# A two-block transformer kernel on one core: norm boundaries taken one row block at a time

## The chip, the cores and the metric

The kernel runs on one core of a Trainium2 chip. The metric is the device time of one execution in microseconds (us). TensorE (PE) does the matrix products, VectorE (DVE), ScalarE (ACT) and GpSimd (POOL) the rest, and SyncE (SP) issues the loads of weights.

## The reference, cut to what matters

Two blocks run one after the other on an x of 512 tokens by 1024 features, all in float32. Each has projections, mixers, gates and a projection back onto the residual. The change touches what stands between them, the root-mean-square norms:

```python
def rms_norm(x, g):
    xf = x.astype(jnp.float32)
    y = xf * lax.rsqrt(jnp.mean(xf * xf, axis=-1, keepdims=True) + EPS)
    return (y * g.astype(jnp.float32)).astype(x.dtype)

# first block
h = rms_norm(x, g_pre_mix);  ...            # "norm1"
x = x + rms_norm(merged @ w_o, g_post_mix)  # post norm "post1"
hf = rms_norm(x, g_pre_ffn)                 # "norm2"
f_gate, f_up = jnp.split(hf @ w_ffn_in, 2, axis=-1)
f = (jax.nn.silu(f_gate) * f_up) @ w_ffn_out
x = x + rms_norm(f, g_post_ffn)             # post norm "post2"
# second block, for l in 0, 1
h = rmsnorm(x, norm_w) * (1.0 + scale[:, None, :]) + shift[:, None, :]   # "layer"
...
x = x + gate[:, None, :] * (merged @ w_out)
# behind it
return rmsnorm(x, final_norm_w)             # "final"
```

## The kernel before

Everything is written out by hand, with semaphores; each engine runs its instructions strictly in the order of the code. A matrix product of float32 accuracy is made of three passes over rounded high parts and low remainders. A weight panel of 1024 by 512 comes as two halves into `raw`. For each half ScalarE makes the high part (`split_hi`, 128x2048) and VectorE the remainder (`split_lo`, 128x2048, semaphore `w_lo`); `w_lo` releases both TensorE and the next load into that half.

The tokens lie in four row blocks of 128 (`tb` 0 to 3). `xres` holds x, and `row0` (shown as R) the rows on their way through a norm. PSUM has eight banks, used as two sets: set 0 is banks 0 to 3, set 1 banks 4 to 7. `set_free[S]` tells TensorE that a set may be written again.

There are four boundaries that the change touches. In the text they are called **A** (`w_o`, then `norm2`), **B** (`ffn_down`, then the first `layer.norm`), **C** (`w_out` of layer 0, then `layer.norm` of layer 1) and **D** (`w_out` of layer 1, then the final norm and the output). At each, TensorE finishes the second 512 columns of a product bank by bank (the order is called `stagger`: banks of blocks 0 and 1, then, after the first halves of blocks 2 and 3, those of blocks 2 and 3). At A and B each row block then goes through this chain between ScalarE and VectorE (`post_norm`, once for each engine):

1. half square sum of the product (`second_half` on ScalarE; at B VectorE first adds up the product in `stage`, `second_half` on VectorE),
2. its mean (`post_variance`, L1137), its root on ScalarE (`post_root`, L655), and beside it the gain (`second_gained`),
3. reciprocal and residual addition (`post_add`, L1146 and L1147, 128x1024),
4. square sum of x (`post_square`, L627), mean (`variance`, L1112), root (`root`, L632), reciprocal (`inverse`, L1118),
5. scaled rows into `row0` (`scaled`, L637, semaphore `xn_ready`).

At C and D the chain is shorter: `update` (two VectorE instructions, L1738 and L1739), half square (`second_half`, L650), mean (L1137), root, inverse, scaled. The split of one more weight half (`split_hi(c.g + 2, 0)` and `split_lo(c.g + 2, 0)`) stands in the middle of each chain. On TensorE `norm_transposes` (L1871) turns the scaled rows: 8 transposes of 128x128 for each block, 4 into each set. Behind them ScalarE reads the banks (`norm_hi` L644 at A, `modulated` L971 at B and C) from the first transpose of block 3 on (the eighth from the end), since `rows_done` counts those of block 3. At D VectorE multiplies the scaled rows with the gain (L1768) and SyncE writes them out.

Two waits of `norm_transposes` matter: at A, set 1 is given free only behind the whole `post_norm` of VectorE; at B, set 0 by `second_half(3)` of VectorE and set 1 long before; at C, set 1 behind `update(1, 3)`.

## Time and profile before

| | before |
|---|---|
| median of 3 runs | 2818.04 us (2817.92 to 2820.89) |
| the profiled execution | 2815.42 us |
| its span, first to last instruction | 2813.7 us |
| PE busy | 2662.9 us, 95% |
| DVE busy | 1210.3 us, 43% |
| ACT busy | 973.6 us, 35% |
| mean granted clock of TensorE | 0.972 of full |

The span is what the trace covers; the execution's own time is 1.7 us more. A busy TensorE is the rule here, so the stretches in which it stands still are the ones to look at.

### The profile page before, as it was taken

The numbers are of one execution on the slowest core, as the hardware profiler recorded it, in microseconds if no ns is written. First come the engines' busy times: TensorE is split into PE (matmuls) and PEld (weight loads), VectorE is DVE, ScalarE is ACT, GpSimd is POOL, SyncE is SP. The second block draws the span as 40 slices with busy tenths as digits, with TensorE's granted clock in tenths as the row PEclk, the third lists the DMA queues.
The fourth block names the chain that finished last, engine by engine and source line by source line (L and its number), as shares of the span: only waits on it lengthen the run. The fifth ranks groups of instructions, "written<-read, shape, count | busy, mean of one in ns | idle before, by whom it ended". The sixth has DMA issues, their size and how long they took to land.

```text
span 2813.7 us, 34747 instructions
## 1 busy us (share of the span) xinstructions
PE 2662.9 (95%) x13629; PEld 2246.0 (80%) x13629; DVE 1210.3 (43%) x1592; ACT 973.6 (35%) x1244; POOL 406.5 (14%) x433
## 2 busy tenths in 40 slices
PE   7999999999997999997999999998999999999897
PEld 6887778777886888886888888987778888888785
DVE  5445555545534655525233333442343332443334
ACT  6335443145324212114333332222343333322233
POOL 3013344000000000000301002321030000123200
PEclk9989999999998999998999999999999999999998
DMA  5220003312431554422322232212222222322221
GB/s 209 75 75 16 16 6 112 105 64 90 149 120 60 183 186 169 149 90 68 112 90 89 89 112 96 93 66 90 75 85 96 89 95 89 128 73 89 80 94 55
DMA packets 43488, 269.26 MB, mean 96 GB/s; under 512 B 5304, under 2 KB 5424, under 8 KB 16000
## 3 DMA queue, kind: packets, MB, share of 16 engines
q1 hardware_dynamic: 31536, 226.51, 23.4%
q0 software_dynamic: 11280, 39.31, 4.1%
q10 hardware_dynamic: 576, 2.10, 0.2%
q8 instruction: 68, 1.11, 0.2%
q14 instruction: 28, 0.23, 0.0%
HBM read 265.80 MB, written 2.10 MB: 95 GB/s over the span
## 4 chain that ended last, share of the span: by engine, by line
PE 68%; issue 19%; DVE 6%; POOL 4%; ACT 3%; DMA 0%; DVEq 0%; POOLq 0%; ACTq 0%
PE PS L1775 66%; POOL merged L578 1%; DVE w_split L1090 1%; PE PS L1981 1%; ACT w_split L614 1%; POOL res_hi L572 1%; POOL res_lo L572 1%; POOL merged L517 1%; DVE small L1335 0%; PE PS L1871 0%; DVE R L1423 0%; DVE h_act L1098 0%; DVE xres L1147 0%; ACT R L627 0%; POOL R L601 0%
## 5 line engine op out<-in xcount | busy, mean ns | idle before, releaser
L1775 PE MATMUL PS<-h_act,w_split 128*128 128x512 f32 x5472 | 1262.1, 392 | 12.2 <-DVEq L1102 7.2
L1775 PEld LDWEIGHTS PS<-h_act,w_split 128*128 128x128 f32 x5472 | 1033.3, 189 | 229.5 <-issue 5.6
L1090 DVE TENSOR_TENSOR w_split<-raw,w_split 128x2048 fp32r<-128x2048 f32 x215 | 508.7, 2366 | 981.0 <-ACT w_split L614 964.8
L614 ACT ACTIVATE w_split<-raw 128x2048 fp32r<-128x2048 f32 x215 | 411.6, 1915 | 835.2 <-PE PS L1775 828.1
L1775 PE MATMUL PS<-w_split,h_act 128*128 128x256 f32 (+2 forms) x2496 | 429.2, 325 | 24.9 <-DVE h_act L1098 19.9
L1775 PEld LDWEIGHTS PS<-w_split,h_act 128*128 128x128 f32 x2496 | 359.1, 193 | 54.3 <-DVE h_act L1098 14.0
L1775 PE MATMUL PS<-y_act,w_split 128*128 128x512 f32 x1152 | 265.2, 391 | 2.2 <-DVE w_split L1090 2.2
L1775 PEld LDWEIGHTS PS<-y_act,w_split 128*128 128x128 f32 x1152 | 217.3, 189 | 47.8 <-DVE w_split L1090 2.6
L1775 PE MATMUL PS<-R 128*128 128x128 f32 (+3 forms) x896 | 189.4, 362 | 9.7 <-ACT R L997 5.5
L1775 PEld LDWEIGHTS PS<-R 128*128 128x128 f32 x896 | 134.3, 200 | 41.6 <-issue 15.0
L1775 PE MATMUL PS<-w_split,res_hi 128*128 128x384 f32 x512 | 130.6, 336 | 0.0
L1775 PE MATMUL PS<-w_split,y_act 128*128 128x512 f32 x528 | 122.5, 394 | 7.8 <-DVE y_act L1098 6.9
L1775 PEld LDWEIGHTS PS<-w_split,y_act 128*128 128x128 f32 x528 | 100.0, 190 | 30.4 <-issue 5.7
L517 POOL TENSOR_TENSOR merged<-merged,small 128x256 f32<-128x256 f32 (+2 forms) x96 | 88.3, 920 | 222.1 <-DVE small L1344 221.8
L578 POOL TENSOR_TENSOR merged<-merged,small 128x768 f32<-128x768 f32 x32 | 46.3, 1469 | 473.5 <-DVE small L1637 473.5
L818 ACT ACTIVATE merged<-PS,small 128x128 f32<-128x128 f32 (+3 forms) x128 | 66.9, 525 | 108.1 <-DVE small L1335 108.1
L614 ACT ACT_TABLE_LOAD x22 | 28.2, 1283 | 207.7 <-PE PS L1775 207.7
L697 ACT ACTIVATE stage<-PS 128x512 f32<-128x512 f32 x94 | 56.0, 598 | 108.2 <-PE PS L1775 108.0
L1775 PEld LDWEIGHTS PS<-w_split,res_hi 128*128 128x128 f32 x512 | 92.0, 188 | 0.0
L1335 DVE TENSOR_REDUCE small<-PS 128x2 f32<-128x256 f32 (+2 forms) x96 | 57.7, 601 | 69.0 <-PE PS L1775 68.6
L1775 PE MATMUL PS<-w_split,res_lo 128*128 128x384 f32 x256 | 85.6, 334 | 0.0
L572 POOL TENSOR_TENSOR res_hi<-h_act,cf 128x512 fp32r<-128x512 f32 x16 | 28.6, 1786 | 333.8 <-DVE h_act L1098 333.8
(274 smaller groups left out, 2143.4 us busy)
## 6 DMA issues: line engine op xcount, KB each, us to landing
raw<-in_weights SPq DMA_DIRECT2D x214, 1024.0 KB, 4.9
R<-in_w_ada POOLq DMA_DIRECT2D x36, 512.0 KB, 4.8
gate_bc<-in_w_ada POOLq DMA_DIRECT2D x12, 512.0 KB, 4.6
xres<-in_x ACTq DMA_DIRECT2D x4, 512.0 KB, 5.6
R<-in_nsa_wk POOLq DMA_DIRECT2D x1, 2048.0 KB, 10.3
xres<-in_x POOLq DMA_DIRECT2D x1, 2048.0 KB, 10.8
R<-in_decay POOLq DMA_DIRECT2D x8, 256.0 KB, 2.9
out<-R SPq DMA_DIRECT2D x4, 512.0 KB, 3.0
```

The source lines that it names most:

```text
L517: pool.tensor_tensor(probs, probs, nsa_fac[:, u % 4, 0:n].unsqueeze(2).to_broadcast([P, n, nk]), ALU.mult).then_inc(p_ready, 1)
L572: pool.tensor_tensor(residue_tiles[part][kt].rearrange("p (r i) -> p r i", r=RES), source, ones, ALU.mult).then_inc(residues_ready, 1)
L578: pool.tensor_tensor(Pa[r], Pa[r], fac[:, r:r + 1].to_broadcast([P, 768]), ALU.mult).then_inc(a_p, 1)
L614: act.activation(w_split[:, 0, half, :, :], raw[:, half, :, :], ACT.Copy).then_inc(w_hi, 1)
L697: act.activation(stage[:, slot0 + j, :], PS[:, 4 * S + j, :], func).then_inc(staged, 1)
L818: last = act.activation(Pn[:, u % 3, k * nk:(k + 1) * nk], PS[:, 4 + u % 2, k * nk:(k + 1) * nk], ACT.Exp, bias=nsa_nmx[:, u % 4, k:k + 1] ...
L1090: dve.tensor_tensor(w_split[:, 1, half, :, :], raw[:, half, :, :], w_split[:, 0, half, :, :].bitcast(F32), ALU.subtract).then_inc(w_lo, 1)
L1335: dve.reduce_max(nsa_nmx[:, u % 4, 0:n], PS[:, 4 + u % 2, 0:n * (qb + 1) * P] .rearrange("p (b k) -> p b k", b=n), AX, negate=True).then_i ...
L1775: return pe.matmul(out, lhsT, rhs, start=start, stop=stop, skip_group_check=True)
L1981: last = pe.transpose(PS[:, 6, k * P:(k + 1) * P], Pn[:, u % 3, k * P:(k + 1) * P], ident)
```

## The change

On ScalarE a root of one spare element (`root_table`) stands ahead of each chain. Both chains now take block 0 to the end of its residual addition before block 1 begins, and blocks 2 and 3 likewise. `split_lo(c.g + 2, 0)` becomes two instructions of 128x1024: the first in the old place, the second behind the last residual addition. In `norm_transposes` only blocks 0 and 1 are written to one set before the other; blocks 2 and 3 are each written to both. The parameter `first` is never passed.

```diff
+            def root_table():
+                act.activation(spare, cf[:, C_ONE:C_ONE + 1], ACT.Sqrt)
...
             def post_norm(posts, k, rows, second_half, ahead):
 
+                root_table()
                 second_half(0)
+                post_root(posts, 0)
                 second_half(1)
-                post_root(posts, 0)
+                post_square(posts, 0)
                 post_root(posts, 1)
-                post_square(posts, 0)
+                root(k, 0)
+                scaled(rows, 0)
                 post_square(posts, 1)
-                root(k, 0)
                 root(k, 1)
-                scaled(rows, 0)
+                scaled(rows, 1)
                 ahead()
-                scaled(rows, 1)
                 second_half(2)
                 post_root(posts, 2)
+                post_square(posts, 2)
                 second_half(3)
                 post_root(posts, 3)
-                post_square(posts, 2)
                 root(k, 2)
+                scaled(rows, 2)
                 post_square(posts, 3)
-                scaled(rows, 2)
                 root(k, 3)
                 scaled(rows, 3)
...
+                root_table()
                 second_half(0)
+                root(k, 0)
                 second_half(1)
-                root(k, 0)
+                scaled(rows, 0)
                 root(k, 1)
-                scaled(rows, 0)
                 scaled(rows, 1)
                 split_hi(c.g + 2, 0)
...
+            def split_lo_part(g, half, part):
+                two = slice(2 * part, 2 * part + 2)
+                dve.wait_ge(w_hi, 2 * g + half + 1)
+                ins = dve.tensor_tensor(w_split[:, 1, half, two, :], raw[:, half, two, :],
+                                        w_split[:, 0, half, two, :].bitcast(F32), ALU.subtract)
+                if part:
+                    ins.then_inc(w_lo, 1)
...
-            def post_norm(own, posts, k, rows, second_half, second_gained, ahead):
+            def post_norm(own, posts, k, rows, second_half, second_gained, g):
 
                 second_half(0)
-                second_half(1)
                 post_variance(posts, 0)
                 second_gained(0)
+                post_add(own, posts, 0)
+                second_half(1)
                 post_variance(posts, 1)
                 second_gained(1)
-                post_add(own, posts, 0)
+                variance(rows, 0)
                 post_add(own, posts, 1)
-                variance(rows, 0)
+                inverse(k, rows, 0)
                 variance(rows, 1)
-                inverse(k, rows, 0)
                 inverse(k, rows, 1)
-                ahead()
+                split_lo_part(g, 0, 0)
                 second_half(2)
                 post_variance(posts, 2)
                 second_gained(2)
                 post_add(own, posts, 2)
                 second_half(3)
                 post_variance(posts, 3)
+                variance(rows, 2)
                 second_gained(3)
-                variance(rows, 2)
                 post_add(own, posts, 3)
+                split_lo_part(g, 0, 1)
                 inverse(k, rows, 2)
                 variance(rows, 3)
                 inverse(k, rows, 3)
...
                 update(1, 0, x_ready)
+                mean(0)
+                inverse(k, rows, 0)
                 update(1, 1, x_ready)
-                mean(0)
                 mean(1)
-                inverse(k, rows, 0)
                 inverse(k, rows, 1)
-                split_lo(c.g + 2, 0)
+                split_lo_part(c.g + 2, 0, 0)
                 update(1, 2, x_ready)
                 mean(2)
                 inverse(k, rows, 2)
                 update(1, 3, x_ready)
+                split_lo_part(c.g + 2, 0, 1)
                 dve.sem_inc(set_free[1], 1)
                 mean(3)
                 inverse(k, rows, 3)
...
-            def norm_transposes(c, rows):
+            def norm_transposes(c, rows, first=0):
...
-                for S in range(2):
+                for S in (first, 1 - first):
                     pe.wait_ge(set_free[S], (c.u0, c.u1)[S])
-                    for tb in range(TB - 1):
+                    for tb in range(2):
                         pe.wait_ge(xn_ready, rows + tb + 1)
                         row(tb, S)
-                pe.wait_ge(xn_ready, rows + TB)
-                row(TB - 1, 0)
-                row(TB - 1, 1)
+                for tb in range(2, TB):
+                    pe.wait_ge(xn_ready, rows + tb + 1)
+                    row(tb, 0)
+                    row(tb, 1)
```

Three places in the order of instructions. First ScalarE at B, from the block-0 and block-1 part's end to the last scaled rows. Before (L614 is `split_hi`, L961 the half square, L655 `post_root`, L627 `post_square`, L632 `root`, L637 `scaled`):

```order
L614 ACTIVATE w_split<-raw 128x2048
L637 ACTIVATE R<-xres,small 128x1024
L961 ACTIVATE merged,small<-stage 128x512
L655 ACTIVATE small<-small 128x1
L961 ACTIVATE merged,small<-stage 128x512
L655 ACTIVATE small<-small 128x1
L627 ACTIVATE R,small<-xres 128x1024
L632 ACTIVATE small<-small 128x1
L627 ACTIVATE R,small<-xres 128x1024
L637 ACTIVATE R<-xres,small 128x1024
L632 ACTIVATE small<-small 128x1
L637 ACTIVATE R<-xres,small 128x1024
```

Of the change (L615, L966, L656, L628, L633 and L638 are the same in this order):

```order
L638 ACTIVATE R<-xres,small 128x1024
L615 ACTIVATE w_split<-raw 128x2048
L966 ACTIVATE merged,small<-stage 128x512
L656 ACTIVATE small<-small 128x1
L628 ACTIVATE R,small<-xres 128x1024
L966 ACTIVATE merged,small<-stage 128x512
L656 ACTIVATE small<-small 128x1
L633 ACTIVATE small<-small 128x1
L638 ACTIVATE R<-xres,small 128x1024
L628 ACTIVATE R,small<-xres 128x1024
L633 ACTIVATE small<-small 128x1
L638 ACTIVATE R<-xres,small 128x1024
```

The split moved behind the scaled rows of block 1; the 128x1024 square of block 2 stands ahead of the half square of block 3, and the scaled rows of block 2 ahead of the square of block 3.

Then VectorE at B, from `second_half(3)` (L1597) to the last reciprocal. Before (L1603 is `second_gained`):

```order
L1597 TENSOR_TENSOR stage<-PS,R 128x512
L1137 SCALAR_TENSOR_TENSOR small<-small 128x1
L1603 TENSOR_TENSOR R<-stage,R 128x512
L1112 TENSOR_SCALAR small<-small 128x1
L1146 RECIPROCAL small<-small 128x1
L1147 SCALAR_TENSOR_TENSOR xres<-R,small,xres 128x1024
L1118 RECIPROCAL small<-small 128x1
L1112 TENSOR_SCALAR small<-small 128x1
L1118 RECIPROCAL small<-small 128x1
```

Of the change (L1614 is `second_half`, L1620 `second_gained`, L1163 the residual addition, L1104 `split_lo_part`, L1134 `inverse`):

```order
L1614 TENSOR_TENSOR stage<-PS,R 128x512
L1153 SCALAR_TENSOR_TENSOR small<-small 128x1
L1128 TENSOR_SCALAR small<-small 128x1
L1620 TENSOR_TENSOR R<-stage,R 128x512
L1162 RECIPROCAL small<-small 128x1
L1163 SCALAR_TENSOR_TENSOR xres<-R,small,xres 128x1024
L1104 TENSOR_TENSOR w_split<-raw,w_split 128x1024
L1134 RECIPROCAL small<-small 128x1
L1128 TENSOR_SCALAR small<-small 128x1
L1134 RECIPROCAL small<-small 128x1
```

The second half of the weight split stands between the last residual addition and the reciprocal of block 2, and the mean of block 2 moved ahead of the gain of block 3.

Last TensorE in `norm_transposes` of a layer (B and C); register rows are the waits on `xn_ready`. Before:

```order
L1871 MATMUL PS<-cf,R 128x128 x4
L1877 REGISTER_ALU
L1871 MATMUL PS<-cf,R 128x128 x4
L1877 REGISTER_ALU
L1871 MATMUL PS<-cf,R 128x128 x4
L1875 REGISTER_ALU
L1871 MATMUL PS<-cf,R 128x128 x12
L1879 REGISTER_ALU
L1871 MATMUL PS<-cf,R 128x128 x8
```

Of the change:

```order
L1889 MATMUL PS<-cf,R 128x128 x4
L1895 REGISTER_ALU
L1889 MATMUL PS<-cf,R 128x128 x4
L1893 REGISTER_ALU
L1889 MATMUL PS<-cf,R 128x128 x8
L1898 REGISTER_ALU
L1889 MATMUL PS<-cf,R 128x128 x8
L1898 REGISTER_ALU
L1889 MATMUL PS<-cf,R 128x128 x8
```

Before, set 0 takes blocks 0, 1 and 2 (4, 4 and 4), then set 1 takes the same three (12), then block 3 goes into both (8). Now set 0 takes blocks 0 and 1 (4 and 4), set 1 the same two (8), and blocks 2 and 3 go into both sets, each behind its own wait (8 and 8).

## Rows read from the trace of the kernel before

**Rows 1.** The page: busy time of each engine.

```profile
PE 2662.9 (95%) x13629; PEld 2246.0 (80%) x13629; DVE 1210.3 (43%) x1592; ACT 973.6 (35%) x1244; POOL 406.5 (14%) x433
```

**Rows 2.** The transposes L1871: idle us and times before them, by what ended it.

```profile
  ACT R L637: 31.0, 8
```

**Rows 3.** Timeline at A: start us, us, engine, line, operation [idle before].

```profile
884.38 1.28 ACT L655 ACT_TABLE_LOAD   x1
...
885.67 0.30 ACT L655 ACTIVATE small<-small 128x1 f32<-128x1 f32 x2
...
891.42 1.90 ACT L614 ACTIVATE w_split<-raw 128x2048 fp32r<-128x2048 f32 x1
...
893.35 2.29 DVE L1090 TENSOR_TENSOR w_split<-raw,w_split 128x2048 fp32r<-128x2048 f32 x1 [2.69 <-ACT w_split L614]
...
895.63 0.68 DVE L1511 TENSOR_TENSOR R<-PS,R 128x512 f32<-128x512 f32 x1
...
895.86 0.58 ACT L932 ACTIVATE merged<-PS 128x512 f32<-128x512 f32 x1
...
898.04 1.04 ACT L627 ACTIVATE R<-xres 128x1024 f32<-128x1024 f32 x1
...
899.54 1.28 DVE L1147 SCALAR_TENSOR_TENSOR xres<-R,small,xres 128x1024 f32<-128x1024 f32 x1
...
903.10 4.74 PE L1871 MATMUL PS<-cf,R 128*128 128x128 f32 x24 [7.71 <-ACT R L637]
903.17 0.17 DVE L1118 RECIPROCAL small<-small 128x1 f32<-128x1 f32 x1 [0.98 <-ACT small L632]
903.37 1.15 ACT L637 ACTIVATE R<-xres,small 128x1024 f32<-128x1024 f32 x1 [0.23 <-DVE small L1118]
907.03 4.74 ACT L644 ACTIVATE h_act<-PS,vecs 128x512 fp32r<-128x512 f32 x8 [2.51 <-PE PS L1871]
...
910.88 4.38 PE L1775 MATMUL PS<-h_act,w_split 128*128 128x512 f32 x12 [3.04 <-DVEq L1102]
```

**Rows 4.** Timeline at B.

```profile
1303.91 1.89 ACT L614 ACTIVATE w_split<-raw 128x2048 fp32r<-128x2048 f32 x1
...
1308.05 0.68 DVE L1597 TENSOR_TENSOR stage<-PS,R 128x512 f32<-128x512 f32 x1
...
1312.67 1.96 PE L1871 MATMUL PS<-cf,R 128*128 128x128 f32 x8 [9.22 <-DVEq L1600]
...
1315.07 1.28 DVE L1147 SCALAR_TENSOR_TENSOR xres<-R,small,xres 128x1024 f32<-128x1024 f32 x1
...
1318.63 5.17 PE L1871 MATMUL PS<-cf,R 128*128 128x128 f32 x24 [4.00 <-ACT R L637]
...
1322.56 2.79 ACT L971 ACTIVATE R<-PS,mod_cols 128x512 f32<-128x512 f32 x4 [2.51 <-PE PS L1871]
```

**Rows 5.** Timeline at C.

```profile
2041.54 16.62 PE L1775 MATMUL PS<-w_split,h_act 128*128 128x512 f32 x72 [0.96 <-DVE w_split L1090]
...
2053.33 1.90 ACT L614 ACTIVATE w_split<-raw 128x2048 fp32r<-128x2048 f32 x1
...
2057.47 0.68 DVE L1738 TENSOR_TENSOR stage<-PS,gate_bc 128x512 f32<-128x512 f32 x1
...
2061.50 1.96 PE L1871 MATMUL PS<-cf,R 128*128 128x128 f32 x16 [2.46 <-ACT R L637]
...
2064.60 2.79 ACT L971 ACTIVATE R<-PS,mod_cols 128x512 f32<-128x512 f32 x4 [0.42 <-PE PS L1871]
...
2067.69 5.68 PE L1775 MATMUL PS<-h_act,w_split 128*128 128x512 f32 x17 [2.36 <-ACTq L619]
```

**Rows 6.** Timeline at D.

```profile
2805.24 0.16 DVE L1118 RECIPROCAL small<-small 128x1 f32<-128x1 f32 x1 [0.27 <-ACT small L632]
...
2805.50 4.63 DVE L1768 TENSOR_TENSOR R<-R 128x1024 f32<-128x1024 f32 x4
```

**Rows 7.** Stretch at C: us, busy (instructions) of PE, PEld, DVE, ACT, POOL, PEclk, DMA.

```profile
2068.00:2069.00 1.00, 1.00 (x3) 0.81 (x3) 1.00 (x4) 1.00 (x3) 0.00 (x0) 0.50 0.00 0
```

7 lines of the change are left out of this document (4 added, 3 removed).

## The prediction

> **What bounds the kernel now.** I read the page first: TensorE is busy for 2662.9 us, 95% of the span [rows 1], so only what shortens the stretches in which it stands still, or the tail behind it, can show. Then the view of the transposes L1871: TensorE idled 31.0 us ahead of them, eight times, until scaled rows (L637) came [rows 2]. That is the sum over the norms and all that is to be had there, about 1% of the span. Then the timelines of the four boundaries, which show what is last. At A the scaled rows of block 2 let a run of 24 transposes begin at 903.10, after 7.71 us of idle time, and ScalarE reads the first finished bank at 907.03 [rows 3]. At B the run of 24 begins at 1318.63 and the first read is at 1322.56 [rows 4]. In both, 16 transposes stand ahead of those of block 3 in this run, and with the first of block 3 they take 3.93 us (907.03 - 903.10, and the same at B). At C a run of 16 takes 1.96 us from 2061.50, and the read is at 2064.60 [rows 5]. At D, the end of the program, VectorE starts its four products at 2805.50, as soon as its last reciprocal (2805.24) is done [rows 6]. So at A, B and C the first read of block 3's banks sets when the next product starts; at D the last reciprocal does.
>
> I take the prices from these rows. An element-wise pass of VectorE over 128x1024: 4.63 / 4 = 1.16 us [rows 6]. Split of a whole weight half on VectorE 2.29, on ScalarE 1.90; half square 0.58 and about 0.12 for its accumulator; gain 0.68; addition to x 1.28; square 1.04 and about 0.11; reciprocal 0.17; scaled rows 1.15; root 0.30 / 2, with hand-over 0.2 [rows 3]. Overlaps of 0.1 and hand-overs of 0.04 are put in as the rows have them. Walking the old order with these prices gives the old starts within 0.15 us at all four places, so I walk the new order the same way.
>
> **The change part by part.**
>
> **Table load.** It goes from behind the second half square (884.38 at A) to ahead of the first, where ScalarE waits for TensorE anyway. Once the load of 1.28 us has begun at 884.38 the roots begin at 885.67, so 1.29 us are freed and nothing beyond the load [rows 3]. They are worth something only if blocks 0 and 1 bound what follows. At A they don't: the split of ScalarE stood between the scaled rows of blocks 0 and 1 and now stands behind both, so it starts at 891.22 by my walk, against 891.42. At B the block-wise order even delays it. `second_half(1)` is now queued behind the addition of block 0 on VectorE, the square of block 0 behind `second_half(1)` on ScalarE, and each reciprocal behind the next addition: the split starts at 1305.98 against 1303.91 [rows 4]. At C it can't start before the first halves of TensorE's banks are done; 48 products behind 2041.54 at 16.62 / 72 = 0.231 each that is 2052.6, against 2053.33 [rows 5]. The Trainium skill ("ScalarE: Activation LUTs", section "What ACT_TABLE_LOAD costs") puts a switch at 2.66 us, as the load and a drain behind it of about 1.38. This case's trace does not agree: the root follows the load directly. By the page each of four boundaries could give 1.38 us more, 5.5 in all.
>
> **Weight split in two.** 2.29 becomes 1.16 + 1.16 (+0.03 in sum), and blocks 2 and 3 begin 1.13 us earlier after ScalarE's part. The rest comes behind the last addition. At A: `post_variance(2)` 1.1 us earlier (894.4). At C: `update(1, 2)` starts at 2055.65 against 2057.47, by 0.7 from the split of ScalarE and 1.13 from here. At B: 2.07 late and 1.13 early, so `second_half(2)` starts at 1309.05 against 1308.05 [rows 4].
> `w_lo` comes later by 3.5 us (C) to 10 us (B). The next product reads it behind the transposes: at 910.88 at A, where it comes by 902.0; at C 2067.69 against 2061.0. Only the load of the next panel's first half is queued on SyncE's ring behind it, and that half is first touched by ScalarE after 48 more products (11 us) of the group that follows. I cost both at nothing; without that cover the lateness itself would be paid.
>
> **Tail of the chain, A and B.** This is the part that costs. On ScalarE the square of block 2 (waiting for the addition) is now ahead of the half square of block 3, which ran during the wait before. Behind the last addition there came: square 3, its mean, root, reciprocal, scaled rows of block 3. Now there come: half a split 1.16, reciprocal of block 2, scaled rows of block 2 (1.15), and only then square 3 (1.15), mean, root, reciprocal.
> At A: addition 2 starts at 895.3, the square of block 2 at 896.64, and the half square of block 3 moves from 895.86 to 897.7; so addition 3 starts at 899.55, as before (899.54); half a split to 902.0; reciprocal 2 to 902.1; scaled 2 to 903.25; square 3 to 904.3; mean, root and reciprocal to 904.95. Before, that reciprocal ended at 903.34 [rows 3]. It is the point at which set 1 is given free, so at A the new order of the transposes gives nothing: 8 of set 1, 8 of block 2 and the first of block 3 are again 17 behind it, 3.93 us, so the read is at 908.9 against 907.03. A: **+1.9**.
> At B: addition 3 starts at 1315.8 (before 1315.07), reciprocal 2 is at 1318.2, scaled 2 to 1319.5, square 3 to 1320.55, reciprocal 3 to 1321.2, scaled 3 to 1322.35 (before 1320.05). But here set 1 has long been free, so the 8 of set 1 go into idle time from 1315.3 on, the 8 of block 2 are done by 1321.4, and the first of block 3 runs at once: read at 1322.35 + 0.5 = 1322.85 against 1322.56 [rows 4]. B: **+0.3**. Of 3.93 us of transposes saved, all but 0.5 are spent on the later chain.
>
> **Tail at C and D.** Everything from `update(1, 2)` on is 1.8 us earlier; the second half split delays the last mean by 0.3. At C set 1 is given free behind that split, at 2060.95; 17 transposes at 1.96 / 16 = 0.12 and the first's latency of 0.25 make 2063.3 against 2064.60 [rows 5]. C: **-1.25**. At D the last reciprocal, and with it the four products and the output, come 1.8 - 0.3 = 1.5 earlier [rows 6]. D: **-1.5**.
>
> At norm1 the transposes run in one piece with all rows ready; nothing changes. TensorE's clock is taken as it is: after the restart at C it is granted 0.50, the 1.2 GHz level [rows 7], and 17 products took 5.68 us instead of 17 x 0.231 = 3.93 [rows 5]; at A 12 took 4.38 instead of 2.77, and the 24 transposes 4.74, 0.20 each against 0.12 at C [rows 3, 5]. So a restart costs about 1.7 us at the low level, and I leave that cost where it is.
>
> **Sum:** 1.9 + 0.3 - 1.25 - 1.5 = -0.55 us, so the profiled execution goes from 2815.42 to 2814.9. The median of the runs is 2.6 us above that execution; I carry it over: 2818.04 - 0.55 = 2817.5.
>
> **The rivals.** A measurement of this kernel tells about 0.2% (5.6 us) from no change.
>
> *The forecast, small losses at A and B against small gains at C and D.* Own range: an error of 0.5 in each of the four walks, and the run-to-run spread of 1.5: 2815.5 to 2819.5. Chance 0.78.
>
> *The tails do not lengthen (faster).* If square 3 still came right behind addition 3, the end would keep its old distance from that addition. A would be 0 (899.55 against 899.54). B would be 0.73 late (1315.8 against 1315.07), scaled 3 done at 1320.8 and the read at 1321.3 against 1322.56, -1.3. With C and D that is -4.0: 2814.0. The queues speak against it: on ScalarE scaled 2 stands ahead of square 3 and waits for a reciprocal behind the half split. With the page's 5.5 on top it would be 2808.5, for which nothing in the rows speaks. Chance 0.07, of which 0.03 beyond 0.2%.
>
> *The clock of TensorE (slower).* The idle time at A grows from 7.71 to 9.6 us, and at C a gap of 2.46 us gives way to one that is placed differently, while the transposes come in more pieces. If the low level then lasts twice as long at the three restarts, each pays 1.7 us more: -0.55 + 5.1 = +4.6, 2822.6; if also the transposes of C (24, now at 0.12 each) ran at 0.21 (5.17 / 24 at B), +1.7 to +2 more, over the 0.2% bound. It decides from one restart on (1.7 against 0.55). For it speaks that the level is 0.50 after the gap at C [rows 7]; against it, that the transposes of A and B run at the slow pace already. The Trainium skill's "TensorE: Matmul & The Clock Gate", section "HAM oscillation", tells the same way round: gaps bring the clock down and the restart pays at half rate. Chance 0.12, of which 0.03 beyond 0.2%.
>
> *The opposite at the clock*, one restart of C at the full level: -1.75 more, 2815.7; it lies in the range. Chance 0.03.
>
> So faster 0.04, same 0.92, slower 0.04. The range for 8 in 10, with half of the clock case in it: 2815.0 to 2820.5.
>
> **What would show it.** Right: at A the run of transposes (24 in one) begins 1.9 us later than before, measured from the end of the product; at B 8 more transposes directly behind the first 8, and the first read within 0.5 of before; at C that read 1.25 earlier; at D the four products 1.5 earlier behind the product; table loads ahead of the first half square with nothing waiting. Wrong: a half square of block 3 that still overlaps addition 2; a half split that takes well over 1.2 us; a wait on `w_lo` at a restart; or more products at the low pace behind a restart than the 12 at A and the 17 at C.

## The result, and the profile after

The changed kernel takes 2822.61 us in the median of 20 runs (2819.78 to 2824.67), the kernel before 2818.01 us in 20 runs (2815.19 to 2820.89). The ratio is 1.0016, with a 95% interval of 1.0009 to 1.0023: 4.6 us slower, a small loss that the interval separates from no change, inside the 0.2% that the prediction named. The forecast of 2817.5 us is off by 5.1 us, and 2822.61 lies above the range of 2815.0 to 2820.5. The profiled execution took 2821.88 us with a span of 2820.2, against 2815.42 and 2813.7. Of those 6.5 us in span 2.5 stand ahead of 632 us, a part that varies by up to 3 us between two traces of one kernel (see the last section). Behind it the change costs 4.0 us, and these are what has to be explained.

The page, and the view of the transposes (now L1889), with what ended TensorE's idle time ahead of them:

```profile
PE 2668.0 (95%) x13613; PEld 2249.6 (80%) x13629; DVE 1210.4 (43%) x1596; ACT 975.2 (35%) x1248; POOL 406.4 (14%) x433
```

```profile
  DVEq L1531: 18.5, 2
  ACT R L638: 11.7, 6
...
  DVEq L1617: 10.1, 1
```

The idle time moved from the scaled rows [rows 2] to other releasers, among them VectorE's queue at A (L1531, 9.11 us at A itself) and at B (L1617). PE shows 5.1 us more busy time than in [rows 1] for the same products. A TensorE that does the same work in more busy time is a first sign of its clock.

The four boundaries are measured from a common start, so that what lies ahead of them doesn't count. At B, C and D it is the start of the product's second panel, ahead of which TensorE stands still for 0.96 us. At A the products run on without a break, so the start is that of the first eight transposes, which follow the last product at once. In the kernel before:

```profile
894.35 1.03 PE L1871 MATMUL PS<-cf,R 128*128 128x128 f32 x8
```

In the changed kernel they start at 896.89, 2.54 us later. Its timeline at A (start us, us, engine, line, operation, idle time before):

```profile
877.84 1.28 ACT L663 ACT_TABLE_LOAD   x1
...
896.89 1.04 PE L1889 MATMUL PS<-cf,R 128*128 128x128 f32 x8
...
900.03 0.58 ACT L937 ACTIVATE merged<-PS 128x512 f32<-128x512 f32 x1
...
901.78 1.28 DVE L1163 SCALAR_TENSOR_TENSOR xres<-R,small,xres 128x1024 f32<-128x1024 f32 x1
902.99 1.22 DVE L1104 TENSOR_TENSOR w_split<-raw,w_split 128x1024 fp32r<-128x1024 f32 x1
...
904.31 1.15 ACT L638 ACTIVATE R<-xres,small 128x1024 f32<-128x1024 f32 x1 [3.09 <-DVE small L1134]
...
907.04 5.38 PE L1889 MATMUL PS<-cf,R 128*128 128x128 f32 x24 [9.11 <-DVEq L1531]
...
910.97 4.74 ACT L645 ACTIVATE h_act<-PS,vecs 128x512 fp32r<-128x512 f32 x8 [2.67 <-PE PS L1889]
...
914.82 2.55 PE L1793 MATMUL PS<-h_act,w_split 128*128 128x512 f32 x10 [2.40 <-DVEq L1118]
```

It is the order that the prediction walked. The half square of block 3 (900.03) stands behind the square of block 2, and the last addition (901.78), half a split (902.99), the scaled rows of block 2 (904.31) and the square of block 3 (at 905.37) follow one another. The 24 transposes begin at 907.04 in one run and the first read is at 910.97. Less 2.54 that is 908.43, against 907.03 [rows 3]: **+1.4**, where +1.9 was forecast. The table load (877.84) stands ahead with nothing waiting.

This late read costs nothing in the end. TensorE restarts 1.40 us late (914.82 less 2.54 is 912.28, against 910.88 [rows 3]), but at the full clock. The first 5 us behind the restart, before and after (us, busy time and number of instructions of PE, PEld, DVE, ACT and POOL, granted clock, DMA share, GB/s):

```profile
910.88:915.88 5.00, 5.00 (x16) 4.03 (x17) 4.75 (x6) 2.68 (x3) 0.54 (x1) 0.70 0.00 0
```

```profile
914.82:919.82 5.00, 5.00 (x22) 4.14 (x23) 4.75 (x6) 2.70 (x3) 1.19 (x1) 1.00 0.00 0
```

Six more products at 0.231 us each are 1.4 us: the low stretch that met the first products before lies on transposes and idle time after.

At B the product started at 1292.28 before and at 1294.84 after, 2.56 us later:

```profile
1294.84 7.55 PE L1793 MATMUL PS<-w_split,y_act 128*128 128x512 f32 x32 [0.96 <-DVE w_split L1096]
...
1316.11 3.51 PE L1889 MATMUL PS<-cf,R 128*128 128x128 f32 x16 [10.10 <-DVEq L1617]
...
1321.92 1.24 PE L1889 MATMUL PS<-cf,R 128*128 128x128 f32 x8 [2.30 <-ACT R L638]
...
1324.76 1.97 PE L1889 MATMUL PS<-cf,R 128*128 128x128 f32 x8 [1.61 <-ACT R L638]
1325.28 2.79 ACT L976 ACTIVATE R<-PS,mod_cols 128x512 f32<-128x512 f32 x4 [0.57 <-PE PS L1889]
```

The first read is at 1325.28, less 2.56 is 1322.72 against 1322.56 [rows 4]: **+0.2** (forecast +0.3). The transposes go in three pieces of 16, 8 and 8. The restart is 0.16 us late (1328.37 less 2.56 against 1325.65), and here the clock adds to it: 35 products in the first 10 us at a granted clock of 0.77, against 37 at 0.83 before, about 0.5 us.

At C the product began at 2041.54 before [rows 5]:

```profile
2047.79 1.43 PE L1793 MATMUL PS<-w_split,h_act 128*128 128x512 f32 x5 [0.96 <-DVE w_split L1096]
...
2065.72 1.97 PE L1889 MATMUL PS<-cf,R 128*128 128x128 f32 x16 [0.41 <-DVEq L1779]
...
2066.24 1.22 DVE L1104 TENSOR_TENSOR w_split<-raw,w_split 128x1024 fp32r<-128x1024 f32 x1
...
2067.62 0.33 SPq L462 DMA_DIRECT2D raw<-in_weights  x1
2067.79 0.16 DVE L1134 RECIPROCAL small<-small 128x1 f32<-128x1 f32 x1 [0.27 <-ACT small L633]
...
2069.19 1.09 PE L1889 MATMUL PS<-cf,R 128*128 128x128 f32 x8 [1.51 <-ACT R L638]
2069.56 2.79 ACT L976 ACTIVATE R<-PS,mod_cols 128x512 f32<-128x512 f32 x4 [0.42 <-PE PS L1889]
...
2073.26 0.76 DVE L1631 CAST h_act<-R 128x512 fp32r<-128x512 f32 x2 [5.30 <-ACT R L976]
...
2074.67 5.91 PE L1793 MATMUL PS<-h_act,w_split 128*128 128x512 f32 x13 [4.39 <-DVE h_act L1114]
```

From product to first read it is 21.77 us (2069.56 - 2047.79), against 23.06 [rows 5]: **-1.3** (forecast -1.25). What ends last ahead of the read is not what the walk had: set 1 came free (L1779) before the half split began, the run of 16 was over at 2067.69, and the transposes of block 3 then waited 1.51 us for their scaled rows (2069.19). But the first product behind it starts at 2074.67, that is 26.88 us behind the product's start against 26.15 (2067.69 - 2041.54): the 1.3 us are lost again between the read and the restart. The reason is in the row of VectorE: its first cast (2073.26) comes 3.70 us behind the read.

At D the product started at 2783.93 before:

```profile
2791.74 1.66 PE L1793 MATMUL PS<-w_split,h_act 128*128 128x512 f32 x6 [0.96 <-DVE w_split L1096]
...
2811.97 3.50 DVE L1786 TENSOR_TENSOR R<-R 128x1024 f32<-128x1024 f32 x3
```

From there to VectorE's products it is 20.23 us (2811.97 - 2791.74) against 21.57 (2805.50 [rows 6] - 2783.93): **-1.3** (forecast -1.5).

So the four walks come to 1.4 + 0.2 - 1.3 - 1.3 = -1.0 us, and the kernel is 4.0 us slower behind 632 us. The table below shows where. It gives, for the profiled execution of each kernel, how much longer than in a second trace of the kernel before (`before_again`) each stage took. The stages are cut at the starts of nine of ScalarE's 215 splits of a whole weight half (L614 or L615), which every kernel has in the same order; in `before_again` they start at 631.9, 876.3, 927.7, 1290.7, 1371.1, 2006.6, 2105.5, 2685.6 and 2782.5 us.

```
                 ahead     A      to    B    heads and   C    layer 1  merge and   D    sum behind
                 of A             B          merge of 0       heads    w_out of 1       632 us
before            0.06   0.05   0.00 -0.03    -0.03    0.01    0.01     0.04     -0.02    0.1
after             0.09   0.05   0.01  0.67     3.07    1.84   -1.83     1.49     -1.35    4.0
after_again      -0.03   0.03  -0.03  0.63     3.04    1.74   -1.83     1.49     -1.31    3.7
no_order         -0.01  -0.76   1.66 -3.19     1.94   -0.28    1.21     1.34     -1.30    0.6
no_split         -0.03  -0.03   0.01  0.63     3.06   -0.53    0.11     0.06     -0.54    2.7
root_turn        -0.05  -0.31   0.03 -2.17     1.95   -0.77   -1.89     1.50     -0.55   -2.3
order_alone       0.11   2.04  -1.61  1.02     1.83   -3.15   -0.03     0.03     -0.35   -0.1
late_post         0.06   0.07   0.02  0.03    -0.03    2.63    1.25     1.39     -0.01    5.4
clear_jump        0.15   0.04  -0.05  0.73     3.07   -0.48    0.15     0.07     -0.53    3.2
best             -0.03  -0.74   1.53 -3.19     1.95   -0.81   -1.88     1.47     -0.50   -2.2
delay_1           0.14   0.13  -0.01  0.29    -0.14    0.03   -0.02     0.00     -0.01    0.4
delay_2           0.05   0.01   0.05  1.21     1.82   -2.85   -0.11    -0.03     -0.02    0.1
delay_3           0.01   0.02   0.01  1.20     1.88   -2.85   -0.09    -0.05      0.01    0.1
clear_delay_1     0.05   0.00  -0.01  1.34     1.82   -0.87   -1.91     1.47     -0.51    1.4
clear_delay_2    -0.01   0.03  -0.01  3.55    -0.13   -0.38    0.16     0.06     -0.50    2.8
```

Two traces of one kernel agree within about 0.1 us in every stage from 632 us on (`before`, and `after` with `after_again`), so a difference of 0.5 in one stage means something even where the medians can't tell. Two numbers of the row `after` stand out: 1.84 at C, where the walk gives -1.3, and 3.07 in a stage of 635 us in which the change does nothing.

**C: the cast that came late.** The window view of both kernels (the last two columns are the share of time in which the DMA engines were busy and the GB/s that they moved). The kernel before:

```profile
2060.00:2062.00 2.00, 0.50 (x5) 0.50 (x6) 1.48 (x3) 1.57 (x3) 0.00 (x0) 1.00 0.84 344
2062.00:2064.00 2.00, 1.47 (x14) 1.23 (x12) 0.32 (x2) 1.54 (x4) 0.00 (x0) 1.00 0.07 29
```

The changed kernel:

```profile
2068.00:2070.00 2.00, 0.81 (x7) 0.81 (x8) 0.00 (x0) 1.58 (x2) 0.00 (x0) 1.00 0.54 152
2070.00:2072.00 2.00, 0.28 (x3) 0.05 (x1) 0.00 (x0) 2.00 (x4) 0.00 (x0) 1.00 0.90 373
```

Before, the load of the next weight half (released by `w_lo`) was over when VectorE did its last reciprocal (2062.8) and its program jumped back for the next layer. In the changed kernel `w_lo` is posted by the second part of the split (2066.24 + 1.22 = 2067.46), SyncE issues the load at 2067.62, and it moves 373 GB/s just when VectorE, done at 2067.95, jumps. The same moment in the DMA view, before (a window of 0.3 us) and then after:

```profile
q14 instruction: 1, 0.01, 7.5%
```

```profile
q1 hardware_dynamic: 15, 0.12, 96.2%
q14 instruction: 1, 0.01, 6.4%
```

The packet of the instruction queue came about 1 us behind the last reciprocal before, and 3.4 us behind it after, amid a load that held the DMA engines 96% of the time. Each cast follows such a packet by about 1.9 us (2065.83 and 2073.26), here and in all other traces. VectorE's own branch shows the same gap. It stands at the head of the layer loop, L1608 before and L1625 after, and the next instruction of that line is the first behind it (duration in ns, first and last start in us):

```profile
L1608 DVEq COMPARE_BRANCH  x1: 56/56/56, 2062.9 to 2062.9; - x1
L1608 DVEq FUSED_REGOPS  x1: 63/63/63, 2065.7 to 2065.7; - x1
```

```profile
L1625 DVEq COMPARE_BRANCH  x1: 56/56/56, 2067.9 to 2067.9; - x1
L1625 DVEq FUSED_REGOPS  x1: 63/63/63, 2073.1 to 2073.1; - x1
```

The jump took 2.8 us before and 5.3 after. That the load delayed the packet was at this point a reading; `late_post` and `clear_jump` test it.

**The heads: the clock.** TensorE at the first heads of layer 0, transposes and products of 128x128. Before:

```profile
1411.19 1.50 PE L1775 MATMUL PS<-R 128*128 128x128 f32 x12
```

After:

```profile
1414.44 2.34 PE L1793 MATMUL PS<-R 128*128 128x128 f32 x12
```

And the windows there, before and after:

```profile
1412.00:1417.00 5.00, 5.00 (x48) 5.00 (x47) 0.85 (x2) 2.22 (x3) 0.00 (x0) 1.00 0.02 3
```

```profile
1414.00:1419.00 5.00, 5.00 (x33) 5.00 (x32) 0.85 (x2) 1.19 (x2) 1.19 (x1) 0.66 0.00 0
```

The same 12 products took 1.50 us before and 2.34 after; 48 instructions against 33 in 5 us; the granted clock was 1.00 before and 0.66 after, the mean of stretches at the 2.4 and the 1.2 GHz level. TensorE had no more idle time ahead of these than before (1.95 us behind GpSimd's `merged` in both). The kernel before has two such short stretches in this stage, near 1545 and 1614 us, the changed one four, near 1415, 1483, 1551 and 1620. One of them costs 1.5 to 1.9 us: the stage is 3.07 us longer with two more, and 1.82 to 1.95 us longer in the kernels below that have one more.

The granted clock can be followed through all stages. This table gives how much longer than in `before_again` TensorE was at the 1.2 GHz level in each stage of the table above (us):

```
                 ahead     A      to    B    heads and   C    layer 1  merge and   D
                 of A             B          merge of 0       heads    w_out of 1
before             0.0    0.0    0.0   0.0      0.0     0.0     0.0       0.0     0.0
after              0.0    0.0    0.0   0.0      6.8     3.4    -3.4       3.4     0.4
after_again        0.0    0.0    0.0   0.0      6.8     3.4    -3.4       3.4     0.4
no_order           0.0    0.0    3.4   0.0      3.4     0.0     3.4       3.4     0.6
no_split           0.0    0.0    0.0   3.4      6.8     0.0     0.0       0.0    -0.6
root_turn          0.0    0.0    0.0   0.0      3.4     0.0    -3.4       3.4     1.2
order_alone        0.0    3.4   -3.4   0.0      3.4    -3.4     0.0       0.0    -0.4
late_post          0.0    0.0    0.0   0.0      0.0     3.4     3.4       3.4     1.9
```

Wherever a stage without an edit became longer or shorter by 1.2 to 1.9 us, it was at the low level for 3.4 us more or less. In the heads of the changed kernel the low level lasts 6.8 us longer, TensorE's busy time is 3.06 us longer, and its idle time is that of `before_again` within 0.01 us. So the 3.07 us there are clock and no wait.

### The profile page after: what moved, and what is told of

Same layout as the page of the kernel before. It is cut to its first block, busy times and chain, and to the rows that moved or that the text cites. A ratio compares the mean times of both kernels' runs of the same rounds, so it can differ in the third digit from the quotient of the medians.

```text
span 2820.2 us, 34739 instructions
## 1 busy us (share of the span) xinstructions
PE 2668.0 (95%) x13613; PEld 2249.6 (80%) x13629; DVE 1210.4 (43%) x1596; ACT 975.2 (35%) x1248; POOL 406.4 (14%) x433
## 4 chain that ended last, share of the span: by engine, by line
PE 68%; issue 19%; DVE 6%; POOL 4%; ACT 3%; DMA 0%; DVEq 0%; POOLq 0%; ACTq 0%
PE PS L1793 66%; POOL merged L579 1%; DVE w_split L1096 1%; PE PS L2000 1%; ACT w_split L615 1%; POOL res_lo L573 1%; POOL res_hi L573 1%; POOL merged L518 1%; DVE small L1352 0%; ACT R L628 0%; DVE R L1440 0%; DVE h_act L1114 0%; ACT R L638 0%; POOL R L602 0%; PE PS L2226 0%
## 5 line engine op out<-in xcount | busy, mean ns | idle before, releaser
L1096 DVE TENSOR_TENSOR w_split<-raw,w_split 128x2048 fp32r<-128x2048 f32 x211 | 499.1, 2365 | 970.1 <-ACT w_split L615 954.0
L615 ACT ACTIVATE w_split<-raw 128x2048 fp32r<-128x2048 f32 x215 | 411.7, 1915 | 842.1 <-PE PS L1793 835.0
```

The lines of the kernel that those rows point to most:

```text
L615: act.activation(w_split[:, 0, half, :, :], raw[:, half, :, :], ACT.Copy).then_inc(w_hi, 1)
L1096: dve.tensor_tensor(w_split[:, 1, half, :, :], raw[:, half, :, :], w_split[:, 0, half, :, :].bitcast(F32), ALU.subtract).then_inc(w_lo, 1)
```

## The experiments

All are timed against the kernel before on the same chip; its median was 2818.65 to 2819.60 us in these sets, so the ratios are to be compared, not the times. "Walk" is the sum by the prediction's way of walking the chains.

**no_order: the change with the old order of the chains.** The early root, the split in two and the new transposes stay.

```diff
                 root_table()
                 second_half(0)
-                post_root(posts, 0)
                 second_half(1)
-                post_square(posts, 0)
+                post_root(posts, 0)
                 post_root(posts, 1)
+                post_square(posts, 0)
...
```

> The change with the old order of ScalarE and VectorE in both chains; early root, weight split in two parts and the new order of the transposes stay. Theory 1 (tails plus a load in the way): the order lengthens the tails at A and B, and the late w_lo puts the load of 1 MB onto VectorE's fetch of code at the jump back of the layer loop. By the same walk as in the prediction A -0.85, B -3.4, C -1.25, D -1.5 = -7.0, and +2.4 for the fetch at C stays: -4.6 against before. Theory 2 (the clock's low stretches fall differently, in steps of 1.65 us, whatever the boundaries do): no relation to the walk, anything from -5 to +5, most likely near +4 as with the change.

Measured: 2818.12 us, ratio 0.9992 [0.9983, 1.0001].

**no_split: the change with the split whole and in its old place.**

```diff
-                split_lo_part(g, 0, 0)
+                split_lo(g, 0)
...
-                split_lo_part(g, 0, 1)
```

(and the same at C and D)

> The change with the weight half split in one piece in its old place. Theory 1: by the walk A +1.8, B +0.3, C -0.7, D -0.7 = +0.7 against before, and no delay of VectorE's first cast at C, since the load is through before the jump (cast within 1.3 us of ScalarE's first read, as before). Theory 2: the gap between first read and first cast at C may stay near 3.7 us, and the time is up to 5 us away from +0.7.

Measured: 2822.38 us, ratio 1.0009 [1.0000, 1.0018].

**root_turn: the kernel before with the early root and the new transposes alone.**

```diff
             def post_norm(posts, k, rows, second_half, ahead):
+                root_table()
...
-                    for tb in range(TB - 1):
+                    for tb in range(2):
```

> Only the early root and the new order of the transposes on top of the kernel before. Theory 1: A -0.45, B -2.5, C -0.7, D -0.7 = -4.3 against before. Theory 2: within 5 us of no change, without relation to -4.3.

Measured: 2816.89 us, ratio 0.9989 [0.9980, 0.9998].

**order_alone: the kernel before with the block-wise order alone.** No early root, whole splits, old transposes.

> Only the block-wise order of ScalarE and VectorE on top of the kernel before; the table is loaded behind the first half square. Theory 1: A +1.35, B +1.55, C -0.3, D -0.3 = +2.4 against before. Theory 2: within 5 us of no change, without relation to +2.4.

Measured: 2817.65 us, ratio 0.9994 [0.9985, 1.0003].

What follows from these four. The order of the chains is the costly part: without it (`no_order`) the ratio is 0.9992 instead of 1.0016, some 7 us, and the sum behind 632 us 0.6 instead of 4.0. At the first read the walk holds in all of them, within 0.7 us. This is how much later than in the kernel before it came, with the walk in brackets (us):

```
                  A               B               C
after         +1.4 (+1.9)     +0.2 (+0.3)     -1.3 (-1.25)
no_order      -1.0 (-0.85)    -3.3 (-3.4)     -1.3 (-1.25)
no_split      +1.3 (+1.8)     +0.1 (+0.3)     -0.5 (-0.7)
root_turn     -0.6 (-0.45)    -2.4 (-2.5)     -0.5 (-0.7)
order_alone   +0.7 (+1.35)    +1.1 (+1.55)    -0.1 (-0.3)
```

So the block-wise order costs 2.4 us at A and 3.5 us at B (`after` against `no_order`) and gains nothing at C, where both are at -1.3. The gain at C comes from the early root with the new transposes (-0.5 in `root_turn`) and the split in two (the other 0.8 of `after`).

The sums don't hold: -4.6 was expected and 0.6 came behind 632 us for `no_order`, +0.7 and 2.7 for `no_split`, -4.3 and -2.3 for `root_turn`, +2.4 and -0.1 for `order_alone`. What lies between is the clock. `no_order` has +1.66, +1.94, +1.21 and +1.34 in four stages that hold no boundary, each with 3.4 us more at the low level. `order_alone` has 3.4 us more of it at A and in the heads (+2.04 and +1.83), and 3.4 us less behind A and at C (-1.61 and -3.15). So edits don't add up in the time, and a walk at the boundaries misses the sums of these kernels by 2 to 5 us.

At C the kernels with the whole split (`no_split`, `root_turn`) show -0.5 to -0.8. `no_order` has the late `w_lo` and a first cast 3.56 us behind the read; its restart is 26.73 us behind the product, late too, and 57 products follow in 15 us at a granted clock of 0.85. Its stage still comes to -0.28, because the 14 us from 2010.8 on, ahead of the product, hold 38 products at 0.76 where the kernel before has 30 at 0.63 (from 2006).

**late_post: the kernel before with `w_lo` posted late at C and D.** The split is whole and in its old place; a copy of its last 8 columns posts `w_lo` behind the last `update`.

```diff
-                split_lo(c.g + 2, 0)
+                split_lo_early(c.g + 2, 0)       # the same, without the post
...
                 update(1, 3, x_ready)
+                post_w_lo(0)                     # 128x8 again, posts w_lo
```

> The kernel before, with w_lo at C and D posted late: the weight half is split in one piece in its old place, and a copy of its last 8 columns behind update(1, 3) posts w_lo. Theory 1: nothing moves but the load of 1 MB, which now starts as VectorE jumps back: its first cast at C comes more than 3 us behind ScalarE's first read (1.2 before), +2 to +2.5 us at the restart of C, no other change. Theory 2 (the late cast at C came from VectorE's longer or shifted code, not from the load): the cast stays about 1.2 us behind the read.

Measured: 2824.34 us, ratio 1.0013 [1.0004, 1.0022]. Its timeline at C:

```profile
2066.42 0.16 DVE L1101 TENSOR_TENSOR w_split<-raw,w_split 128x8 fp32r<-128x8 f32 x1
...
2066.75 0.33 SPq L461 DMA_DIRECT2D raw<-in_weights  x1
...
2069.49 2.78 ACT L971 ACTIVATE R<-PS,mod_cols 128x512 f32<-128x512 f32 x4 [0.42 <-PE PS L1883]
...
2073.10 0.76 DVE L1625 CAST h_act<-R 128x512 fp32r<-128x512 f32 x2 [5.21 <-ACT R L971]
...
2074.52 0.80 PE L1787 MATMUL PS<-h_act,w_split 128*128 128x512 f32 x1 [4.30 <-DVE h_act L1109]
```

The order, the root and the transposes are those of the kernel before, and from product to first read it takes 23.08 us, as before (23.06). Yet the first cast comes 3.61 us behind the read instead of 1.23, and the restart 28.11 us behind the product instead of 26.15: 2.0 us for the time of the post alone. The jump takes 5.2 us. In all 16 traces it takes 5.1 to 5.3 us where the load was issued within 1.1 us ahead of it (`after`, `after_again`, `no_order`, `late_post`) and 2.8 to 3.1 us where it was issued 5 us or more ahead. Behind the restart of C this kernel loses 3.3 us more, in stages with 3.4 us more at the low level each. So one late post costs 5.4 us behind 632 us, more than the 4.0 of the whole change, and only 2.0 of it are wait.

**after_again and before_again: both kernels once more.**

> The changed kernel once more, for a second trace and time. Theory 1: A +1.4, B +0.2 and C and D -1.3 each come back within 0.3, so does the cast 3.7 us behind the first read at C; what differs between the two traces elsewhere comes in steps of about 1.65 us where the clock's low stretch meets a run of products. The time is +3 to +5 against before. Theory 2: A, B, C or D differ by over 1 us from the first trace.

> The kernel before once more, for a second trace and as a test of what two sets of runs of one kernel differ by. Within 1 us (0.04%) of the runs of before; the first profiled execution (2815.42) lies 2.6 us under the median of its kernel, so a second trace should be longer by low stretches of the clock, in steps of 1.65 us, at places that the change doesn't touch.

Measured: 2823.12 us, ratio 1.0015 [1.0006, 1.0024], and 2818.41 us, ratio 0.9997 [0.9988, 1.0006]. The loss repeats, and stage for stage as well (the table above). The expectation for `before_again` was wrong on one point: behind 632 us no low stretch of the clock moved between the two traces.

**clear_jump: the change with the split whole in its old place at C and D only.** There the load is over before the jump; A and B are untouched.

```diff
                 inverse(k, rows, 1)
-                split_lo_part(c.g + 2, 0, 0)
+                split_lo(c.g + 2, 0)
                 update(1, 2, x_ready)
...
                 update(1, 3, x_ready)
-                split_lo_part(c.g + 2, 0, 1)
```

> The change with the weight half split in one piece at C and D alone, so that w_lo and the load of 1 MB come before VectorE's jump. Theory 1: the cast at C is again about 1.25 us behind the first read, the restart of C 25.7 us behind the product (26.8 with the change), and the stage from before C to behind it 2.3 to 2.6 us shorter than with the change (-0.5 to -0.8 against before); A and B as with the change; D 0.8 later than with it.

Measured: 2822.15 us, ratio 1.0013 [1.0004, 1.0023]. Timeline at C:

```profile
2060.76 0.33 SPq L462 DMA_DIRECT2D raw<-in_weights  x1
...
2067.64 2.79 ACT L976 ACTIVATE R<-PS,mod_cols 128x512 f32<-128x512 f32 x4 [0.42 <-PE PS L1888]
2068.86 0.76 DVE L1631 CAST h_act<-R 128x512 fp32r<-128x512 f32 x2 [2.83 <-ACT R L976]
...
2070.82 4.38 PE L1792 MATMUL PS<-h_act,w_split 128*128 128x512 f32 x11 [2.46 <-ACTq L620]
```

The cast is back at 1.22 us behind the read, the jump takes 2.8 us, and the stage C is at -0.48 instead of +1.84: 2.3 us less. It is the counterpart of `late_post`: the load issued 6.9 us ahead of the read instead of 1.9, and the fetch isn't late. But the stages behind it gave 1.4 us back (layer 1 and its merge come to +0.22 instead of -0.34, D to -0.53 instead of -1.35, of which 0.8 is the whole split's own), so the sum is only 0.9 lower, and the ratio 1.0013 against 1.0016 and 1.0015.

Part of C is clock as well. The 15 us behind the restart in the kernel before, and in the changed one:

```profile
2067.70:2082.70 15.00, 15.00 (x59) 12.30 (x60) 8.17 (x14) 6.77 (x7) 9.20 (x6) 0.89 0.21 71
```

```profile
2074.70:2089.70 15.00, 15.00 (x54) 12.14 (x55) 8.35 (x14) 3.55 (x3) 8.78 (x6) 0.81 0.21 71
```

54 products against 59 at a granted clock of 0.81 against 0.89. Five products at 0.231 us (16.62 / 72 [rows 5]) are 1.2 us; the table gives 1.1, the 1.84 of the stage less the 0.73 by which the restart is late. `clear_jump` has 59 again (2070.8 to 2085.8, 0.89). TensorE is idle for 4.39 us ahead of this restart instead of 2.36 [rows 5], but how long it was idle doesn't decide the clock behind it: `root_turn`, with 2.45 us of idle time and no late fetch, has 55 products at 0.82. That the low clock follows from the delay is therefore not shown; that it comes on top of the 2.0 us is.

**delay_1, delay_2 and delay_3: the kernel before with one, two or three needless VectorE passes at B.** Each takes the maximum of 128x1024 of `stage` with itself, ahead of `inverse(k, rows, 2)`; nothing else changes.

```diff
                 post_add(own, posts, 3)
+                if posts:
+                    for _ in range(1):           # 2 and 3 in the others
+                        own.link(dve.tensor_tensor(stage[:, 0:2, :], stage[:, 0:2, :], stage[:, 0:2, :], ALU.max))
                 inverse(k, rows, 2)
```

> The kernel before with one needless pass of VectorE over 128x1024 of stage (1.2 us) behind the last residual addition at B, and nothing else. The square of block 3 on ScalarE covers about 1.0 of it: B +0.2 at the first read. Theory 2b (the clock's low stretches lie on a grid of their own, and a small shift moves which restart meets one): in the heads of layer 0 the time may jump by a whole step of 1.65 us or not at all, with no waits added there. Theory 3 (the heads got slower for another reason of the change's code): 0.0 in the heads.

> The same with two such passes, each behind the other: B +1.4 at the first read. Theory 2b: together with the first and the third, at least one shows a jump by a multiple of 1.65 us in a stage behind B that no instruction of it touches, not in proportion to the delay. Theory 3: everything behind B moves by the delay alone.

> The same with three passes: B +2.6 at the first read. Theory 2b as above; Theory 3: everything behind B moves by 2.6 and the stages behind it keep their length within 0.1 us.

Measured, one run each: 2818.01, 2821.00 and 2818.34 us (the kernel before 2818.65 in the median of 13); single runs that differ by 3 us say nothing, so the stages must. They do. Two passes put 1.21 us on B, the heads, in which nothing was touched, take 1.82 more, and C gives 2.85 back. One pass (0.29 at B) leaves the heads alone. A third pass delays the first read at B by 2.8 us (1.3 with two, 0.3 with one), yet the stage is no longer than with two: behind the restart 44 products run in 10 us at the full clock, against 37 at 0.83 in the others. The two stages that moved, the heads and C, hold 3.4 us more and 3.4 us less of the low level. A shift of the program by 1.2 us changes where the clock falls.

**clear_delay_1 and clear_delay_2: clear_jump with one or two such passes at B.**

> clear_jump with one needless pass of VectorE (1.25 us) ahead of the reciprocal of block 2 at B, where nothing covers it. Theory 2b (the clock's low stretches): the first read at B comes 1.25 us later, but the heads of layer 0, which hold four low stretches with the change and two before, lose one or two of them, so that the stage from B to before C is 1.65 or 3.3 us shorter than in clear_jump and the sum behind B is not longer, perhaps shorter. Theory 3 (another reason in the changed code): the heads stay +3.07 against before and the sum is 1.25 us worse.

> The same with two passes (2.5 us). Theory 2b: steps of 1.65 again, not in proportion. Theory 3: heads +3.07 and the sum 2.5 us worse than clear_jump.

Measured: 2821.18 us, ratio 1.0006 [0.9997, 1.0016], and 2823.17 us, ratio 1.0012 [1.0003, 1.0022]. With two passes B is 2.8 us longer than in `clear_jump`, and the heads are 3.2 us shorter (-0.13 against 3.07). TensorE at the first heads of `clear_delay_2`:

```profile
1420.39 1.50 PE L1795 MATMUL PS<-R 128*128 128x128 f32 x12
```

These are the 1.50 us of the kernel before, in a kernel that has all of the change up to this place, and two passes more. So the 3 us in the heads are not a cost of the order, the split, the root or the transposes as such: they come from where these put the products in time. With one pass, `clear_delay_1` is shorter than `clear_jump` by 1.8 us behind 632 us, though it does more work and waits longer at B.

**best: each boundary with what its walk favours, and no load in the way of the jump.** The early root and new transposes everywhere; at A and B the old order with the split in two; at C and D the block-wise order with the whole split.

```diff
                 second_half(0)
-                post_root(posts, 0)
                 second_half(1)
-                post_square(posts, 0)
+                post_root(posts, 0)
                 post_root(posts, 1)
+                post_square(posts, 0)
...
-                split_lo_part(c.g + 2, 0, 0)
+                split_lo(c.g + 2, 0)
...
-                split_lo_part(c.g + 2, 0, 1)
```

> What the experiments point to: early root and new order of the transposes everywhere; at A and B the old order of ScalarE and VectorE with the weight split in two parts; at C and D the block-wise order with the split in one piece. By the walk A -0.85, B -3.4, C -0.7, D -0.7 = -5.7 against before, and no load in the way of the jump. Theory 1: -4 to -6. Theory 2 (the clock takes part of it back): -1.5 to -3.

Measured: 2815.76 us, ratio 0.9989 [0.9980, 0.9998], faster than both kernels, by about 3 us against the kernel before. `root_turn`, with a third of the edits, has the same ratio, so nothing shows that the rest of `best` adds to it. The walk gave -5.7, and behind 632 us it is -2.2.

## Why the prediction was wrong

**The walk of the chains: right.** At the first read, or the last reciprocal, the four boundaries came at +1.4, +0.2, -1.3 and -1.3 for +1.9, +0.3, -1.25 and -1.5; -1.0 in sum for -0.55. What was to be gained and lost by the order itself was read rightly from the rows, down to the half square of block 3 that no longer overlaps addition 2. The table load gave nothing at A and B, as forecast. At C the number is right by luck. The step says "At C set 1 is given free behind that split, at 2060.95", with 17 transposes to come. The trace shows set 1 free before the half split, 1.6 us earlier than that (its transposes begin at 2065.72, less 6.25 is 2059.47), and the scaled rows of block 3 as what came last. Both paths end at the same time.

**The late `w_lo`: wrong.** The step says: "Only the load of the next panel's first half is queued on SyncE's ring behind it, and that half is first touched by ScalarE after 48 more products (11 us) of the group that follows. I cost both at nothing". The load is indeed early enough for its reader. But it is also work on the DMA engines at a moment that I didn't look at: VectorE's jump back to the head of the layer loop, whose code is fetched over the same engines. It was issued 16.2 us behind the start of the product at C before (at 2057.72) and 19.8 us behind it after, and those 3.7 us put it there. `late_post` measures it alone, 2.0 us at the restart; `clear_jump` takes it away. The walk's -1.3 at C became +0.7 at the restart, and +1.8 with the low clock behind it. The prediction's sentence on what would be wrong named "a wait on `w_lo` at a restart"; it was VectorE's own start that was late.

**The clock: wrong.** The step says: "TensorE's clock is taken as it is", and for the cost of a restart "I leave that cost where it is". The two tables set the account. Of the 4.0 us the walks are -1.0 and the fetch at C is 2.0. The other 3.0 are clock: 1.1 behind the restart of C, 3.1 in the heads, -1.4 behind the restart of A, 0.5 behind that of B, and -0.3 in layer 1 and its merge together. Most of it lies in a stage that the prediction doesn't mention. The rival "the clock of TensorE (slower)" with +4.6 and 2822.6 us named the mechanism and hit the number, but by chance: it put 1.7 us on each restart of A, B and C, and A gained 1.4 instead, B lost 0.5, C 1.1 and the heads 3.1. Its chance of 0.12 was too low. I took the pattern of the clock as fixed, and it was a term of both signs and of steps larger than the walk's sum.

**The range: too narrow.** With a sum of -0.55 from four terms of up to 1.9, and a step of 1.7 that any of many places can gain or lose, 3.0 us upward was too tight a bound. The experiments show shifts of -3.2 to +3.1 in single stages.

What stays open: why the clock falls at the heads in one alignment and not in another (the runs show that it depends on the shift, not by what rule), and why the restart of C is at the low level for longer in some kernels, late fetch or not.

## What to carry to other kernels

When a semaphore also releases a load, a later post moves the load: look at what else is on the DMA engines then, above all at the code fetch of an engine that jumps back in a loop. When the walks sum to less than about 3 us on a TensorE-bound kernel, compare stage by stage with two traces of each kernel and look for low-clock stretches in stages that weren't touched, and don't credit or blame an edit for them. Interleaved chains should be taken apart block by block only where the last block's chain doesn't get longer: at A and B it did, by 2.4 and 3.5 us, and at C nothing was gained by it.

## What the runs showed of the hardware

- A backward jump of VectorE in a loop took 2.8 to 3.1 us, and 5.1 to 5.3 us with a 1 MB load issued within 1.1 us ahead of it. A fetch of instruction code came 3.4 us behind VectorE's last instruction while a 1 MB load was running, and about 1 us without one; the first cast came 3.6 to 3.7 us behind the first read instead of 1.2.
- From 632 us on two traces of one kernel agree within about 0.1 us in each stage, low-clock stretches included; what differs between them is the first 632 us, by up to 3 us. In these two pairs the clock's pattern there belongs to the program, not to the run; for the runs that weren't traced this isn't shown.
- A needless wait can pay: 2.8 us more at B made the heads 3.2 us shorter (`clear_delay_2`), and two needless passes in the kernel before cost 1.2 at B and 1.8 in the heads and gave 2.85 back at C (`delay_2`). With a third the restart at B came 2.8 us late instead of 1.3 and the stage was no longer (`delay_3`).
